# Feed-forward layers of an encoder in float32: second product by seven half products instead of eight, one stream of weight factors, weight sums made in DRAM

## What is computed

```python
def swiglu(xn, w_in, w_out):
    gu = xn @ w_in
    g = gu[..., :FF]
    u = gu[..., FF:]
    return (jax.nn.silu(g) * u) @ w_out

for i in range(DEPTH):
    xn = rmsnorm(h, norm_mix[i])
    h = h + (mlstm_mixer(xn, ...) if i % 2 == 0 else diff_attn(xn, ...))
    xn = rmsnorm(h, norm_ffn[i])
    h = h + swiglu(xn, ffn_w_in[i], ffn_w_out[i])
return h[:, N_META:]
```

## Time and profile before

| | before |
|---|---|
| median of 3 runs | 1957.88 us |
| the profiled execution | 1957.39 us |
| its span, first to last instruction | 1955.2 us |
| PE busy | 1929.1 us (99%) |
| DVE, POOL, ACT busy | 1159.1, 1020.3, 720.6 us |
| TensorE clock granted | 1.000 |
| DMA | 114.90 MB, mean 59 GB/s |

### The profile page before, as it was taken

The page is one execution under the profiler, slowest core; times in us unless marked ns, Lnnn a source line. Parts: engine busy times, 40 slices in busy tenths (PEclk is TensorE's granted clock), DMA queues, the critical chain, the costliest instruction groups (busy, mean ns, idle before and its releaser), DMA issues.

```text
span 1955.2 us, 30311 instructions
## 1 busy us (share of the span) xinstructions
PE 1929.1 (99%) x11145; PEld 1776.7 (91%) x11145; DVE 1159.1 (59%) x1989; ACT 720.6 (37%) x1448; POOL 1020.3 (52%) x1419
## 2 busy tenths in 40 slices
PE   8999999999999999999999999999999999999999
PEld 7888888899999999999988888888889998998998
DVE  7756465777465265265676666666675662662651
ACT  6333333445143142143234444445462340430431
POOL 4432323358496396396632222222557694683873
PEclk9999999999999999999999999999999999999999
DMA  4111111211221221222211111101211222222213
GB/s 160 44 33 44 43 32 33 78 52 56 80 77 56 74 66 57 73 65 71 68 44 33 34 33 32 32 27 38 60 44 57 87 63 72 69 71 60 80 56 97
DMA packets 214921, 114.90 MB, mean 59 GB/s; under 512 B 7012, under 2 KB 213511, under 8 KB 214551
## 3 DMA queue, kind: packets, MB, share of 16 engines
q1 hardware_dynamic: 212816, 112.62, 19.6%
q10 hardware_dynamic: 1990, 0.76, 0.2%
HBM read 108.57 MB, written 4.78 MB: 58 GB/s over the span
## 4 chain that ended last, share of the span: by engine, by line
PE 87%; DVE 5%; POOL 3%; ACT 2%; issue 2%; DMA 1%; ACTq 0%; DVEq 0%; POOLq 0%
PE ps L648 44%; PE ps L720 29%; PE ps L910 3%; PE ps L1071 2%; PE ps L1039 2%; POOL wl L571 2%; PE ps L890 1%; PE ps L1061 1%; POOL wxl L571 1%; PE ps L973 1%; PE ps L919 1%; PE ps L1003 0%; DVE sx L1351 0%; DVE mx L1866 0%; PE ps L875 0%
## 5 line engine op out<-in xcount | busy, mean ns | idle before, releaser
L558 POOL CAST wh<-raw 128x256 fp32r<-128x256 f32 x428 | 167.9, 432 | 732.8 <-PE ps L648 692.6
L720 PE MATMUL ps<-sx,wh 128*128 128x400 f32 (+1 forms) x1408 | 366.8, 342 | 2.3 <-POOL wl L571 1.2
L571 POOL TENSOR_TENSOR wl<-raw,wh 128x256 fp32r<-128x256 f32 x304 | 276.3, 938 | 157.0 <-ACT wh L2051 157.0
L562 POOL TENSOR_TENSOR wl<-raw,wh 128x256 fp32r<-128x256 f32 x428 | 331.0, 803 | 10.3
L720 PE MATMUL ps<-sx,wxh 128*128 128x400 f32 (+1 forms) x1056 | 275.2, 342 | 4.2 <-DVE ut L1471 4.2
L720 PEld LDWEIGHTS ps<-sx,wh 128*128 128x128 f32 x1408 | 257.6, 188 | 3.7 <-ACT p L2058 2.4
L720 PE MATMUL ps<-sx,wl 128*128 128x400 f32 (+1 forms) x704 | 240.3, 341 | 0.0
L2051 ACT ACTIVATE wh<-raw 128x512 fp32r<-128x512 f32 x176 | 106.2, 626 | 351.3 <-PE ps L648 243.0
L648 PE MATMUL ps<-xh,wh 128*128 128x400 f32 (+3 forms) x768 | 220.3, 363 | 0.0
L648 PE MATMUL ps<-xl,wh 128*128 128x400 f32 (+3 forms) x768 | 211.8, 349 | 0.0
L648 PE MATMUL ps<-xh,wl 128*128 128x400 f32 (+3 forms) x768 | 205.8, 346 | 0.0
(11 more groups left out here) (283 smaller groups left out, 3376.9 us busy)
## 6 DMA issues: line engine op xcount, KB each, us to landing
raw<-in_ffn_w_in_dram SPq DMA_DIRECT2D x154, 256.0 KB, 3.0
raw<-in_ffn_w_out_dram SPq DMA_DIRECT2D x48, 384.0 KB, 3.5
raw<-in_m_w_in_dram SPq DMA_DIRECT2D x24, 512.0 KB, 3.7
raw<-in_d_w_in_dram SPq DMA_DIRECT2D x24, 512.0 KB, 3.7
rawx<-in_ffn_w_in_dram SPq DMA_DIRECT2D x22, 256.0 KB, 3.1
raw<-in_m_w_out_dram SPq DMA_DIRECT2D x8, 512.0 KB, 4.1
raw<-in_ffn_w_out_dram SPq DMA_DIRECT2D x16, 256.0 KB, 2.6
wk<-in_x_prompt_dram SPq DMA_DIRECT2D x4, 512.0 KB, 5.6
```

The costliest lines, as they stand in the source:

```text
L558: ins = pool.tensor_copy(wh[:, slot, c], raw[:, slot, c])
L562: ins = pool.tensor_tensor(wl[:, slot, c], raw[:, slot, c], wh[:, slot, c].bitcast(F32), ALU.subtract)
L571: ins = pool.tensor_tensor(slot_of(j, 1)[:, c], factor(g, j)[:, c], slot_of(j, 0)[:, c].bitcast(F32), ALU.subtract)
L720: mm = pe.matmul(product_bank(g, j, layer), slot_of(j, low_w)[:, k * P:(k + 1) * P], sx[layer][:, k * NPROD + j, low_x, :], start=(j in OP ...
```

## The change

**Second product by seven.** Pairs of hidden tiles (even, odd k tile), pairs of output tiles m and m + 4 (columns of `w_out` left and right of 512), and the two token halves give the same seven-product scheme. 11 pairs are worked off in `OUT_PAIRS`: four groups of two and one of three. DVE makes four differences and seven low parts of each pair of hidden tiles, ACT seven high parts. Each of the seven products of an output job ends with an addition to a half of `h` (`add_out`), reading the bank as it stands.

**One stream.** The 154 first-product factors and 140 output factors of a layer stand in one list, `ORDER`. SP loads factor n into one of seven raw slots, ACT makes its high part, POOL its low part, in one of five slots; output products are woven between the last tile of a pair group and the next tile. The signs of T1, T2 and T4 are turned, so that each weight sum is built by additions only.

**Sums in DRAM.** Four sums per layer of the weight blocks, for both products, are DRAM tensors. SP copies the first term (24 transfers a layer: 512 rows of 2.5 or 3 KB, or 768 or 640 rows of 2 KB), POOL adds others by 24 transfers with `accum_op`. Layer 0's copies stand behind the weight loads of heads 1 to 3 and the projection on SP's queue, its additions behind POOL's splits 9 to 31, the last in the feed-forward part; layer 1's copies stand in layer 0's feed-forward stream (jobs 10 to 33, one each), its additions behind POOL's splits in the attention.

**Around it.** POOL splits the attention's first block behind the third product from the end and then does two of the three memsets; `rope_tables` moves behind the last tile's norm operands; layer 1 keeps `h` packed to 768 columns; results leave in halves of 384 tokens. Loops of SP and POOL over mLSTM heads and attention blocks are written out.

```diff
-GROUPS = (4, 6, 6, 6)
+OUT_PAIRS = ((0, 2), (2, 4), (4, 6), (6, 8), (8, 11))
...
+        if f == FT - 1:
+            jobs.update(zip("abcd", (out_job(4, q) for q in range(4))))
+            order += spread(jobs, "P0 P1 P2 P3 P4 P5 a0 P6 b0 a1 b1 a2 a3 b2 a4 a5 b3 a6 c0 b4 c1 b5 c2 b6 c3 d0 c4 d1 c5 d2 "
+                                  "c6 d3 d4 d5 d6")
+        elif f % 4 == 0 and 0 < f < 20:
+            jobs.update(zip("abcd", (out_job(f // 4 - 1, q) for q in range(4))))
+            order += spread(jobs, "P0 P1 P2 P3 P4 a0 P5 a1 P6 a2 b0 a3 b1 a4 b2 a5 b3 a6 c0 b4 c1 b5 c2 b6 c3 d0 c4 d1 c5 d2 c6")
+        elif f > 4 and f % 4 == 1:
+            jobs["d"] = out_job(f // 4 - 1, 3)
+            order += spread(jobs, "P0 d3 P1 d4 P2 d5 P3 d6 P4 P5 P6")
+        else:
+            order += spread(jobs, "P0 P1 P2 P3 P4 P5 P6")
...
+N_SLOT, N_RAW = 5, 7
+IN_PARTS = ((0, 5), (5, 11), (11, 16), (16, 22))
+OUT_PARTS = ((0, 6), (6, 11))
+PARTS = (("in", 0), ("in", 1), ("out", 0), ("in", 2), ("in", 3), ("out", 1))
...
+            def copy_for_sum(layer, i):
+                part, which = divmod(i, 4)
+                unit = N_PART * layer + part
+                if which == 0 and unit > 1:
+                    sp.wait_ge(sums_copied[unit % 2], 64 * (unit // 2))
+                row, col = ((1, 0), (0, 0), (0, 0), (0, 1))[which]
+                sp.dma_start(sum_columns(layer, (0, 2, 1, 3)[which], part),
+                             weight_columns(layer, row, col, part)).then_inc(sums_copied[unit % 2], 16)
...
+            def ffn_factors(layer):
+                for n, (s, j) in enumerate(ORDER):
+                    factor(layer, n)
+                    if layer == 0 and j == 0 and 10 <= s < 34:
+                        copy_for_sum(1, s - 10)
...
+            def add_for_sum(layer, i):
...
+                if step < 4:
+                    pool.wait_ge(sums_copied[unit % 2], 64 * (unit // 2 + 1))
+                    which, other = ((0, weight_columns(layer, 1, 1, part)), (2, weight_columns(layer, 1, 0, part)))[step % 2]
+                    pool.dma_start(sum_columns(layer, which, part), other,
+                                   accum_op=ALU.add).then_inc(sums_added[unit % 2], 16)
...
+            def low_parts(layer):
+                for n, (s, j) in enumerate(ORDER):
+                    pool.wait_ge(prod_hi, NF * layer + n + 1)
+                    columns = k_tiles_of(s) * P
+                    for c in pieces(columns):
+                        ins = pool.tensor_tensor(slot_of(n, 1)[:, c], raw_of(n)[:, c], slot_of(n, 0)[:, c].bitcast(F32),
+                                                 ALU.subtract)
+                    ins.then_inc(prod_split, 1)
...
+            for n in range(2, MIX1):
+                split(n, n % 2, n // 2 + 1)
+                if n >= 9:
+                    add_for_sum(0, n - 9)
+            low_parts(0)
...
+            pool.wait_ge(prod_done, NF - 3)
+            split(MIX1, 0, MIX1 // 2 + 1)
+            for x in (at[:, :, :, :], va[:, :, :, :]):
+                pool.memset(x, 0.0).then_inc(attn_zeroed, 1)
+            pool.wait_ge(prod_done, NF)
+            split(MIX1 + 1, 1, MIX1 // 2 + 1)
...
+            def high_part(layer, n):
...
+                if n >= N_SLOT:
+                    sc.wait_ge(prod_done, NF * layer + n - N_SLOT + 1)
...
+                sc.wait_ge(raws_in[n % N_RAW], 16 * (NF // N_RAW * layer + n // N_RAW + 1))
+                columns = k_tiles_of(ORDER[n][0]) * P
+                sc.activation(slot_of(n, 0)[:, 0:columns], raw_of(n)[:, 0:columns], ACT.Copy).then_inc(prod_hi, 1)
...
+                def add_out(s, j):
+                    (m, half), rank = result_of(s, j), RANK[s, j]
+                    ve.wait_ge(prod_done, NF * layer + PLACE[s, j] + 1)
...
+                    part = h[:, m, half_of(layer, half)]
+                    ve.tensor_tensor(part, part, product_bank(layer, s, j),
+                                     ALU.add if result_of(s, j)[0] >= 4 else ALU.subtract).then_inc(out_read, 1)
```

More of the change, by code:

```diff
@@ L96, with in_job, out_job @@
 C11, C22, C12, C21 = 1, 2, 3, 4
-def summed(g, which):
-    f = g % FT
-    early = {(0, C21): 5, (1, C11): 4, (1, C22): 6, (1, C12): 7}
-    return 4 * (g - f) + early.get((f, which), 4 * f + which)
-def pair_groups(layer):
-    first = layer * FT
-    for gi, tiles in enumerate(GROUPS):
-        yield gi, first, tiles, (FFN0, FFN1)[layer] + KT * gi
-        first += tiles
+def in_job(f):
+    return f + 4 * min(max(f - 1, 0) // 4, 4)
+def out_job(group, q):
+    return 38 + q if group == 4 else 8 * group + 5 + q
@@ new lines, with product_order, spread @@
+TILE_OF = {in_job(f): f for f in range(FT)}
+OUT_OF = {out_job(group, q): (group, q) for group in range(5) for q in range(4)}
+def product_order():
+    def spread(jobs, text):
+        return [(jobs[x[0]], int(x[1])) for x in text.split()]
+    order = []
+    for f in range(FT):
+        jobs = {"P": in_job(f)}
+        if f == FT - 1:
[10 more added lines that the diff above has]
+            order += spread(jobs, "P0 P1 P2 P3 P4 P5 P6")
+    return order
@@ new lines, with result_of @@
+ORDER = product_order()
+NF = len(ORDER)
+PLACE = {job: n for n, job in enumerate(ORDER)}
+OUT_ORDER = [(s, j) for s, j in ORDER if s in OUT_OF]
+RANK = {job: n for n, job in enumerate(OUT_ORDER)}
+N_OUT = len(OUT_ORDER)
+ENDS = {3: (0, 0), 4: (1, 1), 5: (0, 1), 6: (1, 0)}
+OUT_HALF = {0: (0, 0), 1: (1, 1), 2: (0, 1), **ENDS}
+LAST_HALVES = [(s, j) for s, j in OUT_ORDER if OUT_OF[s][0] == 4 and j in ENDS]
+LAST_TILES = [(s, j) for s, j in LAST_HALVES if j > 4]
+def result_of(s, j):
+    row, half = OUT_HALF[j]
+    return OUT_OF[s][1] + 4 * row, half
@@ L591, in _ @@
             split(1, 1, 1, wait=False)
-            with pool.Fori(1, FFN0 // 2) as i:
-                for slot in range(2):
-                    split(i * 2 + slot, slot, i + 1)
-            ffn(0)
+            for n in range(2, MIX1):
[3 more added lines that the diff above has]
+            low_parts(0)
             def split_rest(q):
                 n, part = REST1 + q, slice(q * 4 * P, (q + 1) * 4 * P)
-                high, low = flat_wx(wxh)[:, part], flat_wx(wxl)[:, part]
+                high, low = wrh[:, part], wrl[:, part]
                 pool.wait_ge(o_turned, 2 * D_HEADS)
@@ new lines, in ffn @@
+            def ffn(layer):
+                if layer == 1:
+                    first_products()
+                turned = 0
+                for n in range(2 * layer, NF):
+                    s, j = ORDER[n]
+                    product(layer, s, j)
+                    if n == 5 and layer == 0:
+                        sum_squares(2)
+                    elif n == 5:
+                        add_late_squares(3)
+                    while layer == 1 and turned < len(LAST_HALVES) and PLACE[LAST_HALVES[turned]] + 2 <= n:
+                        turn_result(turned)
+                        turned += 1
+                while layer == 1 and turned < len(LAST_HALVES):
+                    turn_result(turned)
+                    turned += 1
@@ L1581, in _ @@
+                if layer == 0:
+                    for i in range(finished, KT):
+                        low_and_squares(i)
+                    lambda_sums()
+                    rope_tables()
+                    lambda_ready()
+                    invert(3)
             ve.memset(ones[:, :], 1.0).then_inc(ones_set, 1)
@@ L2260, in _ @@
+                if layer == 0:
+                    lambda_loads()
+                    for i in range(finished, KT):
+                        high_and_square(i)
+                    sc.wait_ge(lam_sums, 2)
+                    sc.activation(lam[:, 4:6], lam[:, 0:2], ACT.Exp).then_inc(lam_exp, 1)
+                    root(3)
+                else:
+                    for t in range(copied, len(LAST_HALVES)):
+                        copy_result(t)
             with nc.allow_non_contiguous_dma(reason="16 gate columns"):
```

1146 lines of the change are left out of this document (530 added, 616 removed).

## The result

The changed kernel takes **1910.3 us** (median of 4 runs, 1905.7 to 1912.5) beside 1958.0 us of the kernel before on the same chip: ratio **0.975**, 95% interval 0.9738 to 0.9762. The forecast was 1917 us in a range of 1907 to 1944. The profiled execution took 1908.87 us, its span 1907.0 us.

What follows compares the result with a forecast made beforehand. PE's number of matmuls was taken as the bound. From 1957.39 us, -46.2 + 1 + 1 + 3 + 1 - 2 + 1 + 0.5 = -40.7 gave 1916.7, 1917 us on the median's scale; range 1907 to 1944 us.

Steps and rivals of the forecast that it cites:

- Matmuls: Second feed-forward product: 924 instead of 1056 matmuls a layer, 24.1 us less in layer 0 and 22.1 us in layer 1.
- POOL's low parts: Feed-forward: POOL and DVE work added, 82.3 us in 92.1 of PE per four tiles and one output group; +1 us.
- ACT and DVE, +1 at the end of layer 0: Two finished output tiles and their squares meet layer 0's last products: +1 us, ends 0 and 3.
- Copies, +3: Layer 1's DRAM copies in layer 0's feed-forward part, 4.8 us each, make an odd factor load late: +3 us.
- third rival: Copies in layer 0's feed-forward part hold back factor loads; at 8.5 us a copy +41 us, 1955 us; chance 0.09.
- Accumulating transfers, +1: POOL's 48 issues, nearly all behind mixer weight splits, cost it under 3.4 us each; +1 us for blocked waits.
- Seams: Start of layer 1, without weight sums in PE's chain: -2 us; after layer 0, POOL's late attention split and memsets: +1 us.
- The end, +0.5: After the last matmul, addition, transposes and copy work on 384 columns instead of 256: +0.5 us.
- The first: Whole kernel: the forecast itself holds, between 1910 us with all losses at lower ends and 1930 us; chance 0.72.
- The second: Feed-forward parts: POOL becomes the bound, each factor waiting 0.2 us more behind ACT; +26 us, 1942 us; chance 0.12.
- The fourth: Projection and heads: POOL's issue of an accumulating transfer takes 10 us; +86 us, 2003 us; chance 0.04.
- the fifth: Half the gain lost in DVE's and ACT's fixed order, 1 us at each of 20 places; 1937 us; chance 0.03.

## Why the prediction was right, point by point

**What bounds the kernel: right.** PE is 99% busy before and after. 264 matmuls fewer, 48.9 us less of PE.

**Matmuls: right.** Forecast -46.2 us. In layer 0 three matmuls take 0.547 us in the timeline, 0.1823 each against the 0.1828 used. In layer 1 three take 0.520 us, 0.1733 each, so that the 0.1754 used was 1.2% too much. The stretch of 348 in the earlier trace rows lacks no record: its starts are 0.170 to 0.179 us apart, with one gap of 0.28. Over the whole first product of layer 1 the starts were 0.1747 us apart in the mean before the change; all products of layer 1 together have 0.1734 after it, for the same 384 columns. Why wasn't traced. With 0.1734 the second product saves 184.2 - 160.2 = 24.0 us, not 22.1, and the 1848 matmuls that stay save 2.4 us more.

**POOL's low parts: right in the verdict, mis-sized in two ways.** POOL is busy for 79% of layer 0's part (the forecast said some 85%) and PE waited for its low parts 0.5 us in the whole program. The 82.3 us in 92.1 came from two errors, pieces too cheap and the lock counted in full. The margin is real but finite: a third more of POOL's work and POOL is the bound. The rule of the Trainium skill on the shared port, SBUF — State Buffer, section Who interferes with whom, agrees with the pieces' 0.85 us against 0.74, and not with adding the engines' times.

**ACT and DVE, +1 at the end of layer 0: not seen** as a wait; nothing to tell it from 0.

**Loads: right.** 256 KB still land in 3.0 us in the median; beside a copy in the same queue they take up to 9 us, within their slack.

**Copies, +3: measured 0.** The estimate of 4.8 us of the engines a copy was close (4.1 by the queue rows); they land in 7.4 to 8 us when alone, which the forecast's third rival would have read as nearly its point. That step mistook landing for cost: part of the landing time overlaps with other transfers. The share of the DMA engines, 0.80 with copies and loads, is the number to read. By the Trainium skill, DMA: Bandwidth & Descriptors, section Latency and other measured facts, the estimate was 6.8 us a copy and 10 us more in the sum; the rows show 4.1 us of the engines and no cost.

**Accumulating transfers, +1: this is the term that failed, 9.5 us.** The forecast asked only what an issue costs POOL, and was right on that (1.2 to 1.5 us). It took for granted that DMA has room beside the heads and the projection, which by shares of 0.15 and 0.28 it had before. In place of 1 us for blocked waits, loads stuck behind the transfers' packets cost 7.6 to 9.5 us. In the heads' 323 us the share went from 0.43 (without them) to 0.83, 129 us for 16 transfers or 8 us each. The projection has a share of 0.32 without them, 26 us of 81; seven move in it, 7 x 7.9 = 55 us, which makes 81 us of 81, and they are issued closer together than one of them lasts.

**Seams.** After layer 0 PE waited 1.6 us for POOL's split (forecast 0.5); the stretch is +2.5 us where +1 was taken. The start of layer 1 came out better than -2: its part is 34.1 us shorter to the last product, of which 24.0 are matmuls. PE's idle time in it fell by 4.7 us (6.3 to 1.6), and the price of the matmuls that stay makes 2.4. The other 3 us weren't traced.

**The end, +0.5: measured +1.7.**

**Sum.** -48.1 for matmuls, -10.1 more in layer 1, -1.8 more in layer 0, +7.6, +2.5 and +1.7 at the seams: -48.2, the span's difference. The forecast had -40.7. What it didn't count or charged for nothing: 8.1 us in layer 1, 1.8 in layer 0, 1.9 of matmul price and 5 us for POOL, ACT and the copies, 16.8 us. What cost more than its terms: 6.6 us of accumulating transfers, 1.5 after layer 0 and 1.2 at the end, 9.3 us. So the total is only 7.5 us off because errors of both signs half cancel, which is luck; the verdict isn't, since the matmuls decide it. PE's waits, which the forecast wanted under 15 us in all, add up to some 20 us in the whole program, 5.6 of them for the first load and 4.1 in the projection.

**Rivals.** The first, the forecast itself, happened at the very edge of its 1910 to 1930 us. The second and third did not happen, but both mechanisms exist one step away: POOL with a third more work, the copies with twice the bytes or output products a third shorter. The fourth fell with the 1.2 to 1.5 us of an issue, the fifth with PE's waits.

## What to carry to other kernels

Before moving work into transfers, add up the time that they take of all DMA engines in the stretch where they run, by kind: an accumulating transfer is to be counted at twice a copy. Then look at the spacing: a load that is issued while one of them is being moved shares the engines with it packet by packet, on whichever queue it is, so leave the loads that PE needs soon further apart than one such transfer lasts (11 to 18 us here). A landing time is no price, and an issue cost is the smaller half. An edit can be free in its own stage and cost its neighbour, so compare the stretches by fixed marks, the untouched ones too, and see whether one disturbance lies across a mark. And the price of a matmul of one shape can itself differ by a per cent from one kernel to the next (0.1747 and 0.1734 us).

## What the runs showed of the hardware

Accumulating DRAM-to-DRAM transfers took 20.0% of the 16 engines for 69.2 MB, copies of the same bytes 10.4%, and the memory rows show the same 69.2 MB read and written for each kind. Beside them a 512 KB load went from 4.0 to 16.5 us, if one of them was already being moved when it was issued (14.2 to 17.7 us); issued within 0.3 us of one alone it landed in 3.5 to 4.2. In six such microseconds the engines started 482 packets of the load and 495 of the accumulating transfers. The clock fell to 1.2 GHz for about 3 us after single waits of PE of about 2 us, twice in the projection; this added 1.5 us to each wait.
